# The down products of eight middle FFN groups by seven block products, with weight sums made in DRAM

## The chip, the cores and the metric

The kernel runs on one core of one Trainium2 chip. The metric is the time of one launch on the device, in microseconds (us). All data is float32. Engines are called PE (TensorE), PEld (its weight load), DVE (VectorE), ACT (ScalarE), POOL (GpSimd) and SP (SyncE, which only issues transfers).

## The reference

One encoder layer for two request groups that share the weights: 512 frames of a prompt and 8 x 16 frames of running streams, 640 tokens in all, model width 1024. The layer is an FFN half step, a mixer (short convolution and retention) and a second FFN half step, each followed by a layer norm. The change touches the two FFN half steps alone:

```
def swiglu(x, w_up, w_down):            # D_MODEL 1024, D_FF 2816
    a, b = jnp.split(x @ w_up, 2, axis=-1)
    return (jax.nn.silu(a) * b) @ w_down
x = layer_norm(ALPHA * x + 0.5 * swiglu(x, ffn_w_up, ffn_w_down), ln_g, ln_b)
```

## The kernel before

Every float32 operand of a product is split in a high part and a low part (float32r tiles such as `hh` and `hl`, `wh` and `wl`), and each product is three matmuls into one PSUM bank: high x low, low x high, high x high (`mm3`, L878).

The 22 row tiles of h (128 features by 640 tokens each) go in `GROUPS = (2, 4, 4, 4, 4, 4)`. Each of the five later groups is four quads and then a down stretch. A quad (PE L1130, ACT L1614, DVE L2114) makes two tiles of the up products by seven block products, 84 matmuls of 320 columns: its weights come as `qraw`; POOL makes two sums of them (`sums`, L776); ACT copies the high parts (`wqh`) and DVE subtracts the low parts (`wql`), one quad ahead. ACT and DVE combine the results from PSUM in `ct`, DVE multiplies gate and value to h, ACT copies `hh`, DVE subtracts `hl` and frees PE with `h_ready`.

The down product of a group is 4 row tiles of h (128 features) times 512 x 1024 of the down weights, added into `z` (5 tiles of 128 tokens by 1024). In the middle groups (1 to 4 of each FFN, eight in all) `natural` (L939) makes it in two halves of 512 columns: 10 banks, each summed over 4 k tiles, three matmuls each: 120 matmuls of 512 columns, the stationary operand being a 128 x 128 piece of `hh` or `hl`. Six of them (`lead_down`, L1099) stand in the last quad, to cover a wait there. DVE adds each bank to `z` when it is done (`down`, L2272): five adds after each half. The last group of each FFN and the first (2 tiles) go in other ways.

The down weights come in chunks of 128 x 1024, four a middle group, in a ring of `NSPL = 3` slots of SBUF. A chunk is loaded twice: by SP as `raw`, and by POOL's queue as `wh` with the rounding to float32r (`high`, L754); then POOL subtracts the low part in place (`low`, L764, the instruction is L773). A slot is loaded anew when PE has begun the chunk after the one that it holds (`chunk_used`, inside `mm`, L870). All queues are in the order of the program: POOL's in a middle group is

```
high(ck(3))
for part in range(3):
    sums(2 * k)
    low()
sums(2 * k)
low()
```

so that three chunks are split within the first three quads; the fourth waits for its slot. SP issues `qraw` loads and `raw` loads in one queue (`ffn`, L638).

## Time and profile before

| what | us |
|---|---|
| time, median of 3 runs (lowest, highest) | 1780.93 (1778.66, 1781.36) |
| profiled execution, its span from first to last instruction | 1778.3 |
| PE busy in it | 1766.5 |
| DVE, ACT, POOL busy | 1286.1, 653.3, 551.6 |
| a down stretch of a middle group (first matmul after the quads to first matmul of the next quad) | 25.88 |
| the four quads before it, with the six leading down matmuls | 50.60 |

No time of the profiled execution is listed beside its span; the median of the runs lies 2.6 us above that span. PE's busy time counts matmuls as the profile models them, so it is read beside the starts of single matmuls.

### The profile page before, as it was taken

What the parts mean: (1) busy time and instruction counts of PE and PEld (TensorE: products, weight loads), DVE (VectorE), ACT (ScalarE), POOL (GpSimd) and SP (SyncE); (2) the same over time, 40 slices, a digit from 0 to 9 for tenths busy, and PEclk for the clock granted to TensorE, in tenths of its full rate; (3) what the DMA queues carried; (4) which work ended last, traced back from release to release, by engine and by line L of the source; (5) the groups of instructions that cost most, each with busy time, mean ns of one, the idle gap of its engine ahead of it and who ended that gap; (6) DMA issues with size and microseconds to landing.
All of it is one profiled execution on the core that took longest, in us unless ns stands there. A gap on an engine that the chain in (4) does not pass through costs nothing.

```text
span 1778.3 us, 26857 instructions
## 1 busy us (share of the span) xinstructions
PE 1766.5 (99%) x10776; PEld 1653.0 (93%) x10776; DVE 1286.1 (72%) x1708; ACT 653.3 (37%) x1120; POOL 551.6 (31%) x355
## 2 busy tenths in 40 slices
PE   9999999999999999999999999999999999999998
PEld 9989999898999999999998989898989989899997
DVE  7958485678788787777266777767867968485676
ACT  5425233243545454444105050514224325242343
POOL 3424242242232222221242323332343324233331
PEclk9999999999999999999999999999999999999999
DMA  7442423334443333433674858676963442324223
GB/s 275 136 137 72 143 78 130 126 94 178 148 148 127 115 128 99 139 98 95 243 247 159 313 198 296 214 265 222 351 264 118 129 154 86 131 79 135 90 89 107
DMA packets 87259, 282.61 MB, mean 159 GB/s; under 512 B 8672, under 2 KB 9056, under 8 KB 86880
## 3 DMA queue, kind: packets, MB, share of 16 engines
q1 hardware_dynamic: 48096, 172.77, 29.4%
q10 hardware_dynamic: 24784, 56.21, 8.7%
q0 software_dynamic: 14256, 51.91, 8.6%
q8 instruction: 86, 1.41, 0.3%
q14 instruction: 37, 0.30, 0.1%
HBM read 239.63 MB, written 42.28 MB: 159 GB/s over the span
## 4 chain that ended last, share of the span: by engine, by line
PE 94%; DVE 3%; DMA 1%; ACT 1%; issue 1%; DVEq 0%; ACTq 0%
PE ps L872 93%; PE ps L1348 1%; DMA out_ret_sample<-state 1%; DMA state<-in_state_ret 0%; DVE xl L1961 0%; DVE z L2277 0%; DMA opening<-in_opening 0%; DVE z L2380 0%; PE ps L1257 0%; DVE wql L1961 0%; ACT xh L1510 0%; ACT t L1900 0%; DVE t L2010 0%; DVE y L2415 0%; DVE tl L1961 0%
## 5 line engine op out<-in xcount | busy, mean ns | idle before, releaser
L872 PE MATMUL ps<-th,wql 128*128 128x320 f32 x1136 | 351.0, 309 | 0.0
L872 PE MATMUL ps<-th,wqh 128*128 128x320 f32 x1136 | 350.7, 309 | 0.0
L872 PE MATMUL ps<-tl,wqh 128*128 128x320 f32 x1136 | 350.0, 308 | 0.0
L773 POOL TENSOR_TENSOR wl<-raw,wh 128x1024 fp32r<-128x1024 f32 x100 | 262.8, 2628 | 133.9 <-DMA wh<-in_weights 81.8
L1510 ACT ACTIVATE pu<-ps 128x320 f32<-128x320 f32 x213 | 93.2, 438 | 515.8 <-PE ps L872 515.8
L1961 DVE TENSOR_TENSOR wql<-qraw,wqh 128x512 fp32r<-128x512 f32 x213 | 260.0, 1221 | 17.2 <-ACT wqh L1510 17.0
L872 PE MATMUL ps<-xh,wql 128*128 128x320 f32 x852 | 262.7, 308 | 0.2 <-DVE wql L1961 0.2
L872 PE MATMUL ps<-xl,wqh 128*128 128x320 f32 x852 | 262.7, 308 | 0.0
L872 PE MATMUL ps<-xh,wqh 128*128 128x320 f32 x852 | 262.6, 308 | 0.0
L786 POOL TENSOR_TENSOR quad_s<-qraw 128x512 f32<-128x512 f32 x71 | 96.7, 1362 | 478.8 <-DVE wql L1961 412.9
L1961 DVE TENSOR_TENSOR wql<-quad_s,wqh 128x512 fp32r<-128x512 f32 (+1 forms) x213 | 197.5, 927 | 44.2 <-ACT wqh L1510 43.4
L872 PEld LDWEIGHTS ps<-th,wql 128*128 128x128 f32 x1136 | 213.2, 188 | 0.7 <-ACT pu L1510 0.3
L872 PEld LDWEIGHTS ps<-tl,wqh 128*128 128x128 f32 x1136 | 213.3, 188 | 0.4
L872 PEld LDWEIGHTS ps<-th,wqh 128*128 128x128 f32 x1136 | 213.2, 188 | 0.0
L761 POOL DMA_DIRECT2D wh<-in_weights x92 | 51.7, 563 | 457.1 <-PE ps L872 445.1
L1510 ACT ACTIVATE wqh<-quad_s 128x512 fp32r<-128x512 f32 (+1 forms) x213 | 163.8, 769 | 53.5 <-PE ps L872 50.5
L872 PE MATMUL ps<-wh,hl 128*128 128x512 f32 x420 | 163.8, 390 | 0.1
L872 PE MATMUL ps<-wh,hh 128*128 128x512 f32 x420 | 163.7, 390 | 0.0
L872 PE MATMUL ps<-wl,hh 128*128 128x512 f32 x420 | 163.6, 390 | 0.0
L872 PEld LDWEIGHTS ps<-xh,wql 128*128 128x128 f32 x852 | 159.9, 188 | 1.1 <-DVE wql L1961 0.5
L872 PEld LDWEIGHTS ps<-xl,wqh 128*128 128x128 f32 x852 | 160.0, 188 | 0.4
L872 PEld LDWEIGHTS ps<-xh,wqh 128*128 128x128 f32 x852 | 160.0, 188 | 0.0
(246 smaller groups left out, 3446.2 us busy)
## 6 DMA issues: line engine op xcount, KB each, us to landing
qraw<-in_quads SPq DMA_DIRECT2D x142, 512.0 KB, 3.6
raw<-in_weights SPq DMA_DIRECT2D x100, 512.0 KB, 3.9
wh<-in_weights POOLq DMA_DIRECT2D x92, 512.0 KB, 5.3
state<-in_state_ret ACTq DMA_DIRECT2D x32, 512.0 KB, 7.5
out_ret_sample<-state ACTq DMA_DIRECT2D x32, 512.0 KB, 6.4
state<-in_state_ret SPq DMA_DIRECT2D x16, 512.0 KB, 5.7
qk_scratch<-ctp SPq DMA_DIRECT2D x8, 640.0 KB, 5.6
swish_scratch<-ctp SPq DMA_DIRECT2D x6, 640.0 KB, 2.9
```

The source lines that it names most:

```text
L761: pool.dma_start(w_hi(r), a["weights"][c]).then_inc(hi_loaded[r], 16)
L773: pool.tensor_tensor(w_lo(r), w_raw(r), w_hi(r).bitcast(f32), ALU.subtract).then_inc(chunk_split, 1)
L786: pool.tensor_tensor(qs[:, 0, :], qraw[:, c0, 512:1024], qraw[:, c1, 512:1024], ALU.add).then_inc(pool_sums, 1)
L872: ins = nc.tensor.matmul(out, lhs, rhs, start=start, stop=stop, skip_group_check=adds)
L1348: last = nc.tensor.transpose(cols(k, 128, ps[:, b, :]), src, ident[:, :])
L1510: return nc.scalar.activation(out, in_, ACT.Copy, **kw)
L1961: return V.tensor_tensor(out, x, y, op)
```

## The change

In the middle groups the part of the down product that four of the five token tiles take of the down product is made by seven block products, not eight. Of the four row tiles of h, two form the first row block (features) and two the second; the 512 token columns form two column blocks of 256; the weights of a group form blocks A11, A12 (first 512 output columns, first and second row block) and A21, A22. The fifth token tile (128 tokens) stays out of the seven products: its first half is made with A11 and A12, its second with S1, A22 and one difference `d`. The products take sums of h (`n1`, `n2`, `t3`, `t4`, `d`), which DVE makes (2 x 256 or 2 x 128 columns), ACT rounds to high parts and DVE turns into low parts; and sums of weights S1 to S4, which are made in DRAM: ACT's queue copies four base blocks of 512 KB to a scratch tensor, and POOL's queue adds to them in three accumulating transfers (1 MB, 512 KB, 512 KB), each after the one before has landed.

PE runs 108 matmuls a middle group instead of 120, over seven chunks instead of four, in eight banks, with waits for DVE's reading of a bank between accumulations into it (`down_read`). DVE adds 15 results to `z` instead of 10, between the sums of h. The ring has four slots; the room comes from the scratch of the transfer descriptors, cut from its standard size to 2048. POOL's and SP's orders in a middle group are new. The diff, cut to what the prediction speaks of (indentation reduced):

```diff
-NSPL = 3
+NSPL = 4
...
+SPLIT_GROUPS = range(1, len(GROUPS) - 1)
+SPLIT_CHUNKS = ("A11", "S1", "A12", "S2", "S3", "A22", "S4")
+SUMS_KEPT = ("S1", "S3", "S2", "S4")
+SPLIT_BANKS = 8
+FFN_CHUNKS = 4 + 2 + len(SPLIT_CHUNKS) * len(SPLIT_GROUPS) + 4
...
+        def chunk_source(engine, c):
+    if not is_sum(c):
+        return a["weights"][PLAIN[c]]
+    at, what = split_chunk(c)
+    engine.wait_ge(sums_added[{"S1": 0, "S3": 0, "S2": 1, "S4": 2}[what]], 16 * (at + 1))
+    return a["sums"][at, SUMS_KEPT.index(what)]
...
@@ SP, ffn @@
-        for g in range(1, len(GROUPS)):
+        for g in SPLIT_GROUPS:
+            load(1)
+            load_quad(2 * k)
+            load_quad(2 * k)
+            load(1)
+            load_quad(2 * k)
+            load(2)
+            load_quad(2 * k)
-            load(1)
+            load(3)
...
+    def add_first(at):
+        pool.wait_ge(base_copied, 16 * (at + 1))
+        pool.dma_start(a["sums"][at, 0:2].rearrange("m p d -> (m p) d"),
+                       a["sum_add"][at].rearrange("m p d -> (m p) d"), accum_op=ALU.add,
+                       max_dma_last_dim=4 * D).then_inc(sums_added[0], 16)
+    def add_next(at, step):
+        pool.wait_ge(sums_added[step - 1], 16 * (at + 1))
+        pool.dma_start(a["sums"][at, step + 1], a["sums"][at, 0 if step == 1 else 2], accum_op=ALU.add,
+                       max_dma_last_dim=4 * D).then_inc(sums_added[step], 16)
...
@@ GpSimd, ffn @@
+        for g in SPLIT_GROUPS:
+            at = split_after(k, g)
+            high(ck(1))
+            sums(2 * k)
+            add_first(at)
+            low()
+            sums(2 * k)
+            add_next(at, 1)
+            high(ck(2))
+            sums(2 * k)
+            add_next(at, 2)
             high(ck(3))
             low()
+            sums(2 * k)
+            low()
+            low()
+            high(ck(2))
+            low()
+            high(ck(2))
+            low()
+            low()
...
+    def split_lead():
+        pe.wait_ge(h_ready, hr(2))
+        s, b0 = chunk(), bk.at
+        pe.wait_ge(psum_free, b0 + 3 - 7)
+        for kk in range(2):
+            last = mm3(ps[:, (b0 + 3) % 8, :], (hh[:, kk, 0:128], hl[:, kk, 0:128]),
+                       (cols(kk, 512, w_hi(s)), cols(kk, 512, w_lo(s))), kk == 0, kk == 1)
+        last.then_inc(down_full, 1)
+        return s
+    def split_down(led, h0):
+        at, b0 = split_done.at, bk.at
+        y_at, o1, x_at, o2, w_at = (0, 1), 2, (3, 4), 5, (6, 7)
+        def product(s, place, left, start):
+            if start:
+                pe.wait_ge(psum_free, b0 + place - 7)
+            for kk in range(2):
+                last = mm3(ps[:, (b0 + place) % 8, :], (left[0](kk), left[1](kk)),
+                           (cols(kk, 512, w_hi(s)), cols(kk, 512, w_lo(s))), start and kk == 0, kk == 1,
+                           adds=not start)
+            return last
...
+        product(led, x_at[1], of_h(0, 1), True).then_inc(down_full, 1)
+        product(led, o1, of_h(0, 2), True)
+        owed[0] = True
+        s = chunk()
+        summed(1)
+        for q in range(2):
+            product(s, w_at[q], of_sum(n1h, n1l, q), True).then_inc(down_full, 1)
+        product(s, o2, of_h(0, 2), True)
+        owed[0] = True
+        s = chunk()
+        pe.wait_ge(h_ready, h0 + 4)
+        for q in range(2):
+            product(s, y_at[q], of_h(2, q), True).then_inc(down_full, 1)
+        product(s, o1, of_h(2, 2), False).then_inc(down_full, 1)
+        owed[0] = True
+        s = chunk()
+        summed(2)
+        for q in range(2):
+            read(1 + q)
+            product(s, x_at[q], of_sum(n2h, n2l, q), False).then_inc(down_full, 1)
+        owed[0] = True
+        s = chunk()
+        summed(3)
+        for q in range(2):
+            read(5 + q)
+            product(s, x_at[q], of_sum(t3h, t3l, q), False).then_inc(down_full, 1)
+        owed[0] = True
+        s = chunk()
+        summed(5)
+        for q in range(2):
+            read(7 + q)
+            product(s, x_at[q], of_sum(t4h, t4l, q), False).then_inc(down_full, 1)
+        product(s, o2, of_sum(dh, dl, 0), False).then_inc(down_full, 1)
+        owed[0] = True
+        s = chunk()
+        for q in range(2):
+            last = product(s, w_at[q], of_h(2, 3 + q), False)
+            if q == 0:
+                last.then_inc(down_full, 1)
+        last.then_inc(psum_full, SPLIT_BANKS)
+        owed[0] = True
+        bk.add(SPLIT_BANKS)
+        split_done.add()
...
+    def base_copy(at):
+        if at:
+            act.wait_ge(sums_added[0], 16 * at)
+        act.dma_start(a["sums"][at].rearrange("m p d -> (m p) d"),
+                      a["sum_base"][at].rearrange("m p d -> (m p) d")).then_inc(base_copied, 16)
+    def split_his(n):
+        ts_hi_part(n2h, n2f)
+        ts_hi_part(t3h[:, :, :], t3f[:, :, :])
+        ts_hi_part(dh[:, :, :], df[:, :, :])
+        act.wait_ge(h_ready, 2 * (stage_of(n) // 2 + 1) + 2 * (ffn_index(n) // 2 + 1))
+        ts_hi_part(t4h, t4f[:, :, :])
...
@@ ScalarE, quad and ffn @@
...
+        if split_quad(n) and local(n) % 4 == 2:
+            ts_hi_part(n1h[:, :, :], n1f[:, :, :])
...
+        if ends and split_quad(n):
+            split_his(n)
...
+                if q == 2 and g in SPLIT_GROUPS and split_after(k, g) < 2 * len(SPLIT_GROUPS) - 1:
+                    base_copy(split_after(k, g) + 1)
...
+    def ts_lo_part(out, f, hi):
+        ts.add()
+        dve.wait_ge(ts_hi, ts())
+        tt(out, f, hi.bitcast(f32), ALU.subtract).then_inc(ts_ready, 1)
+    def first_difference(n):
+        dve.wait_ge(h_summed, ffn_index(n) // 2)
+        summed_of_h(tt(n1f[:, :, :], h32_first, h32_second, ALU.subtract))
...
+        def out_of(place, t, half, last, sign=1.0):
+            if place == "w1" and last:
+                dve.wait_ge(psum_full, b0 + SPLIT_BANKS)
+            else:
+                seen.add()
+                dve.wait_ge(down_full, seen())
+            zt = cols(half, 512, z[:, t, :])
+            ins = V.scalar_tensor_tensor(out=zt, in0=ps[:, (b0 + places[place]) % 8, :], scalar=sign * scale,
+                                         in1=zt, op0=ALU.mult, op1=ALU.add)
+            if last:
+                ins.then_inc(psum_free, 1)
+            else:
+                read.add()
+                ins.then_inc(down_read, 1)
...
+        dve.wait_ge(h_summed, ffn_index(n) // 2 + 1)
+        summed_of_h(V.scalar_tensor_tensor(out=n2f, in0=n1f[:, :, :], scalar=-1.0, in1=h32_second,
+                                           op0=ALU.mult, op1=ALU.subtract))
+        h_lo_part(n)
+        out_of("x0", 0, 0, False)
+        out_of("x1", 1, 0, False)
+        step(tt(t3f[:, :, :], h32_second, b12[0], ALU.subtract))
+        dve.wait_ge(ts_summed, 5 * at + 2)
+        step(V.scalar_tensor_tensor(out=t4f[:, :, :], in0=n2f, scalar=-1.0, in1=h32_first,
+                                    op0=ALU.mult, op1=ALU.subtract))
+        after()
+        ts_lo_part(n2l, n2f, n2h)
+        out_of("w0", 3, 1, False, -1.0)
+        out_of("w1", 4, 1, False, -1.0)
+        summed_of_h(tt(t3f[:, :, :], t3f[:, :, :], b12[1], ALU.subtract))
+        step(tt(odd_pieces(df[:, :, :]), h32_odd, odd1[0], ALU.subtract))
+        out_of("y0", 0, 0, True)
+        after()
+        summed_of_h(tt(odd_pieces(df[:, :, :]), odd_pieces(df[:, :, :]), odd1[1], ALU.subtract))
+        summed_of_h(V.memset(mv[:, TT, 0:1], 0.0))
+        ts_lo_part(t3l[:, :, :], t3f[:, :, :], t3h[:, :, :])
+        out_of("y1", 1, 0, True)
+        out_of("o1", 2, 0, True)
+        out_of("x0", 3, 0, False)
+        ts_lo_part(dl[:, :, :], df[:, :, :], dh[:, :, :])
+        out_of("x1", 4, 0, False)
+        ts_lo_part(t4l, t4f[:, :, :], t4h)
+        z_settled()
+        out_of("x0", 3, 1, False, -1.0)
+        out_of("x1", 4, 1, False, -1.0)
+        z_settled()
+        out_of("x0", 0, 1, True, -1.0)
+        out_of("x1", 1, 1, True, -1.0)
+        out_of("o2", 2, 1, True)
+        out_of("w0", 3, 0, True)
+        out_of("w1", 4, 0, True)
+        assert (seen.at, read.at) == (15 * at + 15, 8 * at + 8)
+        bk.add(SPLIT_BANKS)
+        dve.wait_ge(psum_free, bk())
+        split_done.add()
     def quad(n):
...
@@ VectorE, quad @@
...
+            if split_quad(n):
+                first_difference(n)
...
+        if split_quad(n) and local(n) % 4 == 2:
+            ts_lo_part(n1l[:, :, :], n1f[:, :, :], n1h[:, :, :])
...
+        if ends and split_quad(n):
+            split_evacuations(n)
         if prepares:
             quad_lo_part(n + 1, A22)
             quad_lo_part(n + 1, S4)
-        if ends and not projects:
+        if ends and not projects and not split_quad(n):
             h_lo_part(n)
...
-            if g < len(GROUPS) - 1:
-                down(0.5 / ALPHA, 0)
-                down(0.5 / ALPHA, 1)
...
+    elif f0 + tiles < FT:
+        part = quarters(down, f0)
+        for what in SPLIT_CHUNKS:
+            if what[0] == "A":
+                out.append(part[what])
+        bases.append([part[of] for of in ("A21", "A21", "A11", "A12")])
+        added.append([part[of] for of in ("A22", "A11")])
...
-    nc = bacc.Bacc("TRN2", target_bir_lowering=False, num_devices=1)
+    nc = bacc.Bacc("TRN2", target_bir_lowering=False, num_devices=1, dynamic_dma_scratch_size=2048)
```

The chunks of a group come in the order A11, S1, A12, S2, S3, A22, S4. `down_full` counts PE's block results, `down_read` DVE's reads of banks that PE adds to again, `ts_summed`, `ts_hi` and `ts_ready` the sums of h, their high parts and their low parts. `base_copy` of the next group is issued by ACT after the third quad of a group.

## Rows read from the trace of the kernel before

**Rows 1.** The page's first part: busy us, share, instructions of each engine.

```profile
PE 1766.5 (99%) x10776; PEld 1653.0 (93%) x10776; DVE 1286.1 (72%) x1708; ACT 653.3 (37%) x1120; POOL 551.6 (31%) x355
```

**Rows 2.** The page's chain that ended last, by engine.

```profile
PE 94%; DVE 3%; DMA 1%; ACT 1%; issue 1%; DVEq 0%; ACTq 0%
```

**Rows 3.** Windows: stretch, busy us of each engine, granted clock, transfers' share, GB/s.

```profile
124.83:175.43 50.60, 50.60 (x343) 50.34 (x342) 40.41 (x42) 24.72 (x42) 19.90 (x12) 1.00 0.30 92
175.43:201.31 25.88, 25.88 (x117) 21.41 (x116) 11.46 (x16) 2.00 (x3) 4.96 (x5) 1.00 0.47 155
...
430.76:1372.58 941.82, 940.02 (x5890) 880.80 (x5888) 685.80 (x1017) 350.47 (x619) 284.05 (x179) 1.00 0.56 191
```

**Rows 4.** Timeline of PE (start, us, instruction) at both ends of that down stretch.

```profile
175.28 0.31 PE L872 MATMUL ps<-xh,wqh 128*128 128x320 f32 x1
175.43 0.39 PE L872 MATMUL ps<-wh,hl 128*128 128x512 f32 x1
...
201.31 0.32 PE L872 MATMUL ps<-xh,wql 128*128 128x320 f32 x1
```

**Rows 5.** Timeline of DVE and of ACT about the start of that down stretch.

```profile
173.93 0.68 DVE L1961 TENSOR_TENSOR wql<-quad_s,wqh 128x512 fp32r<-128x512 f32 x1
174.54 0.68 DVE L1961 TENSOR_TENSOR quad_s<-quad_s,qraw 128x512 f32<-128x512 f32 x1
175.69 0.82 DVE L1961 TENSOR_TENSOR ct<-pu,ps 128x640 f32<-128x640 f32 x1 [0.47 <-issue]
176.54 1.49 DVE L1961 TENSOR_TENSOR ct<-ct,ct 128x1280 f32<-128x1280 f32 x1
...
178.07 1.37 ACT L1510 ACTIVATE hh<-ct 128x640 fp32r<-128x640 f32 x2 [1.80 <-DVE ct L1961]
...
179.16 1.56 DVE L1961 TENSOR_TENSOR hl<-ct,hh 128x640 fp32r<-128x640 f32 x2
```

**Rows 6.** Timeline of POOL about the same start.

```profile
172.17 1.29 POOL L786 TENSOR_TENSOR quad_s<-qraw 128x512 f32<-128x512 f32 x1 [5.04 <-DVE wql L1961]
174.69 1.68 POOL L790 TENSOR_TENSOR quad_s<-qraw 128x512 f32<-128x512 f32 x1 [1.23 <-DVE wql L1961]
181.59 0.57 POOL L761 DMA_DIRECT2D wh<-in_weights  x1 [5.23 <-PE ps L872]
```

**Rows 7.** Timeline of POOL and of DVE, both at work in a quad.

```profile
75.30 2.86 POOL L773 TENSOR_TENSOR wl<-raw,wh 128x1024 fp32r<-128x1024 f32 x1
...
76.65 2.86 DVE L1961 TENSOR_TENSOR ct<-ct,ct 128x1280 f32<-128x1280 f32 x1
```

**Rows 8.** Timeline of POOL and of DVE, both at work in a down stretch.

```profile
105.12 0.58 POOL L761 DMA_DIRECT2D wh<-in_weights  x1 [5.01 <-PE ps L872]
109.89 2.39 POOL L773 TENSOR_TENSOR wl<-raw,wh 128x1024 fp32r<-128x1024 f32 x1 [4.19 <-DMA wh<-in_weights]
...
108.71 3.41 DVE L2277 SCALAR_TENSOR_TENSOR z<-ps,z 128x512 f32<-128x512 f32 x5 [3.87 <-PE ps L872]
```

**Rows 9.** DMA issues of the page: count, KB each, median us to landing.

```profile
qraw<-in_quads SPq DMA_DIRECT2D x142, 512.0 KB, 3.6
raw<-in_weights SPq DMA_DIRECT2D x100, 512.0 KB, 3.9
wh<-in_weights POOLq DMA_DIRECT2D x92, 512.0 KB, 5.3
...
out_y_prompt<-in_ln_b ACTq DMA_DIRECT2D x1, 1024.0 KB, 7.4
out_y_prompt<-y POOLq DMA_DIRECT2D x2, 512.0 KB, 6.9
```

**Rows 10.** Timelines of ACT, DVE and POOL within quads.

```profile
159.86 0.48 DVE L1961 TENSOR_TENSOR ct<-pu,ps 128x320 f32<-128x320 f32 x1
...
162.00 0.44 ACT L1510 ACTIVATE ct<-ps 128x320 f32<-128x320 f32 x1 [0.86 <-PE ps L872]
...
147.04 1.29 POOL L786 TENSOR_TENSOR quad_s<-qraw 128x512 f32<-128x512 f32 x1 [6.49 <-DVE wql L1961]
```

**Rows 11.** Timeline of PE at both ends of the kernel, and the window after it.

```profile
1.26 4.58 PE L872 MATMUL ps<-ones 128*128 128x320 f32 x16 [1.26 <-DVE ones L2470]
...
1769.76 0.39 PE L872 MATMUL ps<-wh_x,hh 128*128 128x512 f32 x1
...
1771.00:1774.00 3.00, 0.00 (x0) 0.00 (x0) 2.72 (x8) 1.54 (x3) 0.00 (x0) 0.96 0.86 341
```

More of the change, by code:

```diff
@@ L60, with split_chunk, is_sum, split_after @@
 RELEASES = release_order()
+def split_chunk(c):
+    for k, at in enumerate((0, CHUNKS - FFN_CHUNKS)):
+        n = c - at - FIRST_UNITS - 2
+        if 0 <= n < len(SPLIT_CHUNKS) * len(SPLIT_GROUPS):
+            return len(SPLIT_GROUPS) * k + n // len(SPLIT_CHUNKS), SPLIT_CHUNKS[n % len(SPLIT_CHUNKS)]
+    return None
+def is_sum(c):
+    return split_chunk(c) is not None and split_chunk(c)[1][0] == "S"
+PLAIN = [sum(not is_sum(e) for e in range(c)) for c in range(CHUNKS)]
+def split_after(k, g):
+    return len(SPLIT_GROUPS) * k + g - 1
+def group_banks(g):
+    return SPLIT_BANKS if g in SPLIT_GROUPS else 2 * TT
+def split_quad(n):
+    return stage_of(n) != 1 and local(n) // 4 + 1 in SPLIT_GROUPS
 def released(c):
@@ L117 @@
 PROJ = QUAD_START[1]
-PROJ_BANKS = 2 * 4 + 3 * QUADS + 2 * TT * len(GROUPS) + 2 * TT + 2 * 4
+PROJ_BANKS = 2 * 4 + 3 * QUADS + sum(group_banks(g) for g in range(len(GROUPS))) + 2 * TT + 2 * 4
 HEADS_BANKS = PROJ_BANKS + 3 * len(PROJECTIONS) + 1 + 2 * 2 + 2 * KT
@@ L495, in build_layer @@
         sig_made, h_summed, h_hi = sem("sig_made"), sem("h_summed"), sem("h_hi")
+        base_copied = sem("base_copied")
+        sums_added = [sem(f"sums_added{n}") for n in range(3)]
+        down_full, down_read = sem("down_full"), sem("down_read")
+        ts_summed, ts_hi, ts_ready = sem("ts_summed"), sem("ts_hi"), sem("ts_ready")
         t_summed, t_hi, t_ready = sem("t_summed"), sem("t_hi"), sem("t_ready")
@@ L1237, in ffn @@
                         first_down()
-                    elif g < len(GROUPS) - 1:
-                        for half in range(2):
-                            natural(tiles // 2, hh, hl, lambda k: pe.wait_ge(h_ready, h0 + k + 1),
-                                    led=None if half else led)
+                    elif g in SPLIT_GROUPS:
+                        split_down(led, h0)
                     else:
@@ L2744, in weight_chunks, with quarters @@
 def weight_chunks(ffn1_up, ffn1_down, w_in, w_conv, w_ret, w_out, ffn2_up, ffn2_down):
-    out = []
+    out, bases, added = [], [], []
+    def quarters(w, f0):
+        return {f"A{d}{k}": tiled(w[(f0 + 2 * k - 2) * 128:(f0 + 2 * k) * 128, (d - 1) * 512:d * 512], 512)
+                for d in (1, 2) for k in (1, 2)}
     def tiled(w, cols):
@@ L2787, in weight_chunks @@
     ffn(ffn2_up, ffn2_down)
-    return np.stack(out)
+    return np.stack(out), np.array(bases), np.array(added)
 def kernel(x_prompt, x_sample, cache_conv, state_ret, ln1_g, ln1_b, ffn1_w_up, ffn1_w_down, w_in, conv_w,
```

101 lines of the change are left out of this document (76 added, 25 removed).

## The prediction

> **What bounds the kernel now.** The page's first part shows PE busy for 1766.5 of 1778.3 us [rows 1], and the chain of waits ends in PE for 94% of the span [rows 2]. The windows say that this holds in every stage that the change touches: in the four quads of a middle group and in its down stretch PE is busy for 50.60 of 50.60 and 25.88 of 25.88 us, at the full granted clock [rows 3]. So matmuls taken away are worth their full time, and so is every wait put in. The same windows give the reserve of the others: in the down stretch DVE works 11.5 of 25.9 us, ACT 2.0, POOL 5.0; in the quads DVE works 40.4 of 50.6. The kernel waits for nothing there, and the question is whether DVE and POOL, which get the new work in the stretch where PE gets shorter, still keep ahead.
>
> **PE's own work.** A down stretch has 114 matmuls of 512 columns between 175.43 and 201.31 [rows 4]: 25.88 / 114 = 0.227 us each. The change takes 12 of 120 away: 2.72 us a group, 21.8 us in eight groups. Counted from the start of the stretch (T), with no wait, PE would begin S1 at 2.7, A12 at 6.8, S2 at 10.9, S3 at 13.6, A22 at 16.3, S4 at 20.4 and end at 23.2 (12, 18, 18, 12, 12, 18, 12 matmuls).
>
> **DVE and POOL hold each other up.** POOL's low part took 2.39 us beside DVE's adds from PSUM, which also ran on at 3.41 / 5 = 0.68 us each [rows 8]. In a quad it was otherwise: POOL's low part began at 75.30 and took 2.86, and DVE's product of two SBUF tiles, issued at 76.65, took 2.86 instead of the 1.49 of the same product at 176.54 [rows 5, 7]. 76.65 + 2.86 - 1.49 = 78.02, when POOL's 75.30 + 2.86 = 78.16 was nearly over. So a DVE instruction with two SBUF inputs waits for a running POOL subtraction, the other way round as well (POOL's 1.68 against 1.29 of the sister sum [rows 6]), and an add from PSUM doesn't.
> This trace agrees with the Trainium skill ("SBUF — State Buffer", section "Who interferes with whom"), which says that a DVE instruction with two SBUF inputs and a GpSimd one that reads SBUF exclude each other for the whole instruction.
>
> **Where POOL now works.** Before, three low parts lie in the quads and POOL is idle from 176.37 to 181.59 [rows 6], just when DVE makes the last two tiles of h [rows 5]. After, the order is sums, low A12, low S2 with nothing to wait for between: sums end at T + 0.9 (176.37 - 175.43), since their second half waits for DVE's subtraction at 173.93 [rows 5, 6]; then two low parts of 2.4 us, alternating with DVE:
> - DVE's product for h needs 1.4 us (176.54 to 177.95 before); it gets in before or behind the first low part and h is there at T + 3.1 to 4.7 instead of 2.5.
> - the new difference n2 (0.61, the distance of the starts at 173.93 and 174.54 [rows 5]) waits for the end of one low part, then DVE's two `hl` subtractions (0.72 each) for the end of the other. Low parts end at about 5.4 and 8.4, so h is ready at 8.4 + 1.5 = 9.9. PE wants it at 6.8: wait 3.1 us. Before it was ready at 180.71 - 175.43 = 5.3 [rows 5].
>
> **DVE's chain to S3.** PE may add S3's products only after DVE has read x0 the second time (`down_read` 5). After `hl` stand eight adds to z (8 x 0.67), five operations on 512 columns (t3 twice, t4, low parts of n2 and t3: 5 x 0.61), two on 256 (0.33 each) and 0.2 of small things: 5.4 + 3.0 + 0.7 + 0.2 = 9.3 us of work, and T + 19.2. In it fall POOL's low S3 and low A22 (the wh transfer is issued at about 8.4, behind the low parts, and lands 4.8 later [rows 8]): 0 to 2.4 us each. Laying the instructions of DVE, POOL, ACT and PE in order with these durations I get 1.1 + 2.4: S3 begins at 22.7 instead of 13.6. The remaining adds keep up with PE, since they come one per 1.36 us of matmuls. Net a group: 9.1 of waits (3.1 before A12, 6.0 before S3) less 2.7 is +6.4 us. The same laying out gives 76.45 a group for the old order, where the trace has 50.60 + 25.88 = 76.48, and DVE's and POOL's starts within 0.3 us. With landings between 4.6 and 6.5 us it gives +6.1 to +9.3; with neither of the last two low parts in the way, +2.8.
>
> **The clock.** A wait of 6 us is new: in this trace the granted clock fell once, after the last matmul at 1769.76 (mean 0.96 in 1771 to 1774), and the first 16 matmuls took 4.58 us, 0.286 each where later ones of the same shape take 0.147: the lower level, 1.2 GHz of 2.4 [rows 11]. So PE's clock may fall before S3; one fall by these rows costs half of 4.58 = 2.3 us. I count half of it, 1.15 us a group (bounds 0 and 2.3).
> The Trainium skill ("TensorE: Matmul & The Clock Gate", section "HAM oscillation — how this bites in real kernels") says that waits of this kind return in every round with their slow matmuls; by it the full price would stand in every group, the second rival below. The trace of before can't show it, as its waits in the groups are none.
>
> **What else is added, counted at nothing.** ACT: five roundings (5 x 0.6 us) in an engine that works 2.0 of 25.9 us, hidden. Third quad: DVE gets n1 and its low part, 1.2 us, ACT 0.54; DVE's result for the last product stands 2.1 us ahead of the copy that comes just before PE's need [rows 10], so 0, at most 0.7 us a group (5 in all). Weight traffic: seven chunks of twice 0.5 MB instead of four, 2 MB of copies and 2 MB of accumulation, in all 8.4 MB -> 15 to 17 MB a group, 113 -> about 200 GB/s; the middle of the kernel moves 191 GB/s with PE at 940 of 942 us [rows 3], so hidden. The three accumulating transfers stand one quad (12.3 us) or more apart; the nearest rows are 6.9 us (accumulating, 0.5 MB) and 7.4 us (1 MB within DRAM) [rows 9], and POOL, which waits for each, is idle 6.5 us before its sums [rows 10]. Held up behind POOL's wait are its sums, and behind SP's wait for S2 the fourth `qraw` load: hidden until a link takes some 19 us. The fourth slot and the smaller scratch: between -3 and +3 us elsewhere, taken as 0.
>
> **Sum.** 8 x (6.4 + 1.15) = +60 us on a span of 1778.3: 1838. The median of the runs is 2.6 above this span: **1841**. This case alone reaches from 8 x 2.8 = +22 (1803) to 8 x (9.3 + 2.3) = +93 (1874).
>
> **Rivals.**
> - *DVE keeps ahead, the change gains* (17%). If the low parts fall on DVE's adds from PSUM, which they don't disturb [rows 8], DVE's work from T to `down_read` 5 is about 14.0 us against PE's 13.6: 0.5 us lost, 2.2 gained a group, 8 x 2.2 = 17.6, **1763**. For it: POOL's lows are 4 x 2.4 in 22 us, DVE's adds leave holes for them. Against: POOL's queue puts two of them on the tiles of h, and no add can be moved there. It decides below 2.7 us of waits a group.
> - *The clock falls at both waits of every group* (11%): 8 x (6.4 + 2 x 2.3) = +88, **1869**. For: the waits are longer than before by far. Against: 3.1 and 6.0 us are short, and only the end of the kernel shows a fall at all.
> - *The accumulating transfers are slow* (6%). If the first takes 25 us, POOL stands 25 - 13.6 = 11.4 us, of which 6.5 are idle time; 4.9 us later reach PE's next quad in every group: 8 x (7.55 + 4.9) = +100, **1881**. For: they read and write the same DRAM and nothing like them is in the trace. Against: 6.9 us for half the size.
> - *Both effects cancel* (4%): waits of just 2.7 us, **1781**.
>
> **How the numbers follow.** The likeliest case has 62%. All cases but the first and last rivals are slower: 79%; within 0.2% (3.6 us, what a measurement of this kernel can tell from none) 4%; faster 17%. The range 1790 to 1875 leaves out the faster case, the even one and part of the slow transfers, and cuts nothing of the likeliest.
>
> **What would show it.** PE's idle time in a middle group by releaser: before the first matmul of A12 a wait for `hl`, about 3 us, and before S3 a wait for a DVE add to z, about 6 us; POOL's wl subtractions right after its last sum, and DVE instructions with two SBUF inputs of 2 to 3 us beside them; 10,680 matmuls; the granted clock in the down stretch below 1.00 if it falls. Down stretches of 23 to 24 us would prove me wrong, as would waits that stand in the quads and not in the down stretch (transfers), or sums of h that don't slow down beside POOL.

## The result and the profile after

The changed kernel takes 1879.8 us (median of 4 runs, 1873.2 to 1880.6) against 1780.2 before (median of 4): **ratio 1.0554, 95% interval 1.0537 to 1.0572**. It is slower by 5.5%. The prediction was 1841 with a range of 1790 to 1875: the direction was right, the size was not, and the time lies outside the range. The profiled execution has a span of 1877.9 us at a mean granted clock of 0.979 (before 1778.3 at 0.999).

The page's first part (busy us, share, instructions), and its chain that ended last:

```profile
PE 1786.2 (95%) x10680; PEld 1654.4 (88%) x10680; DVE 1445.9 (77%) x1860; ACT 674.4 (36%) x1160; POOL 641.2 (34%) x427
...
PE 19%; DVE 10%; DMA 2%; issue 2%; ACT 1%; POOL 0%; DVEq 0%; POOLq 0%; ACTq 0%
```

PE has the 96 matmuls fewer that were counted, 10,680 instead of 10,776 [rows 1], and is yet busy 19.7 us longer: matmuls at the lower clock take longer. DVE is busy 160 us longer. Its new instructions alone make 63 of these (1349.3 us busy in experiment 5, where nothing holds them up, against 1286.1 before); the rest is time in which an instruction of DVE counts as busy and stands held up by POOL. The chain of before was PE for 94% [rows 2]; now it is followed for a third of the span only and goes through DVE and a load of `qraw`.

The windows of the stages [rows 3]: the quads of the second middle group, its down stretch, the down stretch of the last middle group, and the middle of the kernel (busy us of each engine, granted clock, transfers' share, GB/s):

```profile
140.44:191.18 50.74, 50.74 (x343) 50.34 (x342) 40.93 (x45) 25.12 (x43) 17.48 (x14) 1.00 0.70 203
191.18:229.04 37.86, 27.39 (x105) 21.05 (x103) 28.85 (x31) 4.20 (x7) 18.71 (x11) 0.91 0.44 146
1762.09:1793.13 31.04, 25.35 (x105) 19.92 (x103) 27.30 (x32) 4.20 (x7) 18.60 (x12) 0.95 0.59 178
483.36:1429.29 945.93, 942.56 (x5890) 881.77 (x5888) 702.67 (x1017) 350.63 (x619) 280.21 (x178) 1.00 0.55 191
```

Before, a down stretch took 25.88 us with PE always busy; now this one takes 37.86, and PE stands for 10.5 of them. The eight stretches together take 298.1 us instead of 207.0: **+91.1 of the 99.6 us of span**. The middle of the kernel gives +4.1 (945.9 against 941.8), the quads and the rest +4.4. The 91.1 are taken apart by the starts of the matmuls: gaps of more than 0.24 us beyond a matmul's own time (waits) sum to 85.1 us, matmuls that start late by 0.06 to 0.24 us (those at the low clock, called slow matmuls below) to 26.3, 1.5 are small delays, and the twelve matmuls fewer per group take 21.8 away.

**Where PE waits.** PE's waits by releaser (us in total, times, longest):

```profile
PE ps L983 <- DVE z L2372: 36.5, 8, 7.3
PE ps L983 <- DVE ct L2187: 26.9, 9, 4.7
```

The first row is the predicted wait before S3, for DVE's adds to z, eight times. The second wasn't predicted: seven times PE waits 3.2 to 4.9 us (27.6 together) before S1, the second block product, because DVE hasn't read out the last quad's banks (`ct`). T is again the start of the stretch. Timeline of DVE in the stretch that starts at 191.18 (start, us, instruction, idle time before it and its releaser):

```profile
189.78 0.69 DVE L2187 TENSOR_TENSOR wql<-quad_s,wqh 128x512 fp32r<-128x512 f32 x1
195.10 1.73 DVE L2187 TENSOR_TENSOR quad_s<-quad_s,qraw 128x512 f32<-128x512 f32 x1 [4.63 <-POOL quad_s L878]
196.76 0.81 DVE L2187 TENSOR_TENSOR ct<-pu,ps 128x640 f32<-128x640 f32 x1
197.60 2.80 DVE L2187 TENSOR_TENSOR ct<-ct,ct 128x1280 f32<-128x1280 f32 x1
200.44 2.79 DVE L2387 SCALAR_TENSOR_TENSOR ct<-n1f,ct 128x512 f32<-128x512 f32 x1
...
207.13 2.77 DVE L2187 TENSOR_TENSOR n2r<-ct,n2r 128x512 fp32r<-128x512 f32 x1
```

and of POOL in the same stretch:

```profile
193.80 1.26 POOL L878 TENSOR_TENSOR quad_s<-qraw 128x512 f32<-128x512 f32 x1 [9.43 <-DMA qraw<-in_quads]
195.03 1.26 POOL L882 TENSOR_TENSOR quad_s<-qraw 128x512 f32<-128x512 f32 x1
196.24 6.43 POOL L852 TENSOR_TENSOR wl<-raw,wh 128x1024 fp32r<-128x1024 f32 x2
...
206.47 2.89 POOL L852 TENSOR_TENSOR wl<-raw,wh 128x1024 fp32r<-128x1024 f32 x1 [0.37 <-DMA wh<-sums_scratch]
```

Read them together. POOL's sums, which stood at T - 3.3 before [rows 6], start at T + 2.6, since POOL waits 9.4 us for a load. DVE's second sum waits for them, and the read-out of the banks stands behind it in DVE's queue. Then mutual exclusion of DVE's instructions with two SBUF inputs and POOL's subtractions, as predicted: beside POOL's two low parts (6.43 us for two) DVE's product takes 2.80 instead of 1.49 us and the difference n2 2.79 instead of 0.68; beside the third, which begins at 206.47, the low part of n2 takes 2.77.

**The late load.** Transfers: the issues of the page (KB each, median us to landing), and the same for 184 to 186 us alone, where that load is issued:

```profile
qraw<-in_quads SPq DMA_DIRECT2D x142, 512.0 KB, 3.7
...
sums_scratch<-in_sum_add POOLq DMA_DIRECT2D x8, 1024.0 KB, 10.0
```

```profile
qraw<-in_quads SPq DMA_DIRECT2D x1, 512.0 KB, 8.7
```

and for 178 to 190 us:

```profile
sums_scratch<-sums_scratch POOLq DMA_DIRECT2D x1, 512.0 KB, 12.1
wh<-sums_scratch POOLq DMA_DIRECT2D x1, 512.0 KB, 13.2
sums_scratch<-in_sum_base ACTq DMA_DIRECT2D x1, 9.4
```

The 2 MB base copy for the next group is issued at 179.31, the third accumulation at 180.5 and the load of S2, the result of the second, at 181.1. The second half of the fourth `qraw` load follows at 184.96 and lands after 8.7 us instead of 3.6 [rows 9]. It is also issued late, at T - 6.2; before it was T - 7.7. SP waits there for a subtraction of DVE, which POOL's low part of S1 holds up. DVE and then POOL at that time:

```profile
181.76 3.17 DVE L2187 TENSOR_TENSOR wql<-qraw,wqh 128x512 fp32r<-128x512 f32 x1
```

```profile
181.66 2.71 POOL L852 TENSOR_TENSOR wl<-raw,wh 128x1024 fp32r<-128x1024 f32 x1
```

The last group has no copy beside it, and fits this: no wait before S1, 31.04 us, with 3.1 us before A12 (predicted 3.1) and 2.7 before S3. Experiments 2 and 3 test it.

### The profile page after: what moved, and what is told of

Its sections match the earlier page's. It is cut to its first block and busy times, and to the rows that moved or that the text cites. A ratio compares the mean times of both kernels' runs of the same rounds, so it can differ in the third digit from the quotient of the medians.

```text
span 1877.9 us, 27089 instructions
## 1 busy us (share of the span) xinstructions
PE 1786.2 (95%) x10680; PEld 1654.4 (88%) x10680; DVE 1445.9 (77%) x1860; ACT 674.4 (36%) x1160; POOL 641.2 (34%) x427
## 3 DMA queue, kind: packets, MB, share of 16 engines
q0 software_dynamic: 22192, 81.27, 15.7%
## 5 line engine op out<-in xcount | busy, mean ns | idle before, releaser
L852 POOL TENSOR_TENSOR wl<-raw,wh 128x1024 fp32r<-128x1024 f32 x124 | 327.4, 2644 | 146.3 <-DMA wh<-in_weights 48.8
L878 POOL TENSOR_TENSOR quad_s<-qraw 128x512 f32<-128x512 f32 x71 | 98.0, 1380 | 605.8 <-DVE wql L2187 386.8
L983 PE MATMUL ps<-xh,wqh 128*128 128x320 f32 x852 | 262.6, 308 | 0.0
L2187 DVE TENSOR_TENSOR wql<-qraw,wqh 128x512 fp32r<-128x512 f32 x213 | 249.8, 1173 | 0.4
L2187 DVE TENSOR_TENSOR quad_s<-quad_s,qraw 128x512 f32<-128x512 f32 x138 | 114.2, 827 | 54.7 <-POOL quad_s L878 47.7
L882 POOL TENSOR_TENSOR quad_s<-qraw 128x512 f32<-128x512 f32 x71 | 112.5, 1584 | 73.4 <-DVE wql L2187 73.4
L1705 ACT ACTIVATE wqh<-qraw 128x512 fp32r<-128x512 f32 x213 | 132.8, 624 | 10.4 <-PE ps L983 10.4
```

The lines of the kernel that those rows point to most:

```text
L852: pool.tensor_tensor(w_lo(r), w_raw(r), w_hi(r).bitcast(f32), ALU.subtract).then_inc(chunk_split, 1)
L878: pool.tensor_tensor(qs[:, 0, :], qraw[:, c0, 512:1024], qraw[:, c1, 512:1024], ALU.add).then_inc(pool_sums, 1)
L882: pool.tensor_tensor(qs[:, 2, :], qraw[:, c0, 0:512], qraw[:, c0, 512:1024], ALU.add).then_inc(pool_sums, 1)
L983: ins = nc.tensor.matmul(out, lhs, rhs, start=start, stop=stop, skip_group_check=adds)
L1705: return nc.scalar.activation(out, in_, ACT.Copy, **kw)
L2187: return V.tensor_tensor(out, x, y, op)
```

## The experiments

Times are medians with the ratio to the kernel before (1779 to 1780 us on the same chip) and its 95% interval. "Stretches" are the eight down stretches together (before 207.0, after 298.1).

**1. DVE's second sum behind the bank read-out.** In the fourth quad `second_sum` moves behind the products of h.

```
-                    second_sum(n + 2)
+                    if not (ends and split_quad(n)):
+                        second_sum(n + 2)
...
                 if not ends_stage_at(n, 2):
+                    if ends and split_quad(n):
+                        second_sum(n + 2)
                     fourth_sum(n + 2)
```

> In the last quad of a split group DVE's sum for the quad after next (it waits for POOL's sums) is moved behind the reading out of the banks. Theory 1 (POOL's last sums of a group come 4 us late, because their qraw load is late, and DVE stands in front of the last quad's bank until they come): the wait before the S1 products (3.2 to 4.9 us in seven groups, 27.6 us in all) goes, with it one of the two falls of the clock; low parts of A12 and S2 still come late and hold DVE, so about 34 us a down stretch instead of 37.3: 1850 us, between 1838 and 1862. Rival (the S1 wait is set by something else, the bank or the n1 parts): within 5 us of 1880.

1835.2 us, 1.0318 [1.0299, 1.0337], 3 us under the expected range; stretches 257.3. The wait before S1 is gone in all eight groups. Before A12 it is 2.3 to 2.8, before S3 1.5 to 7.3 us. So this queue order carries 45 us of the loss. That is more than the S1 waits (27.6 us), since the waits before S3 got shorter too. What ends these is not always DVE: PE's waits of this kernel, and POOL's low part of S3 in the second group (T = 182.53):

```profile
PE ps L983 <- POOL wl L852: 28.4, 13, 3.0
PE ps L983 <- DVE z L2372: 17.9, 6, 7.2
```

```profile
199.84 2.35 POOL L852 TENSOR_TENSOR wl<-raw,wh 128x1024 fp32r<-128x1024 f32 x1 [4.98 <-DMA wh<-sums_scratch]
```

In five of the eight groups S3 starts when this low part ends (here at T + 19.7; DVE's second reading of x0 had ended at T + 18.6). Its chunk is issued only behind POOL's two low parts, and POOL waits 5.0 us for the landing. So POOL's own lateness is a second way in which its low parts cost time, beside the hold on DVE. (Before A12 the first row names POOL too, but there DVE's `hl` ends later: T + 9.0 against 8.4, with A12 at 9.1.)

**2. The base copy in four pieces, one a quad.**

```
-                if at:
-                    act.wait_ge(sums_added[0], 16 * at)
-                act.dma_start(a["sums"][at]..., a["sum_base"][at]...).then_inc(base_copied, 16)
+                if at > 1:
+                    act.wait_ge(sums_added[0], 16 * (at - 1))
+                act.dma_start(a["sums"][at, m], a["sum_base"][at, m]).then_inc(base_copied[at % 2], 16)
...
```

> The 2 MB base copy of the next group is issued as four copies of 512 KB, one behind each quad, instead of one behind the third. Theory 1 (the copy and the accumulation beside it hold up the qraw load): POOL's last sums are on time, the S1 wait goes in all groups, down stretches are as the one group without a copy, 31 us instead of 38: 7 x 7 = 49 us less, 1831, between 1822 and 1848. Rival (it is SP's queue, where the qraw load stands behind the S2 chunk that waits for an accumulation, and not the bytes in flight): nothing changes, 1875 to 1885.

1860.2 us, 1.0462 [1.0441, 1.0483]; stretches 267.4. A miss by 12 us over the range: the wait before S1 did shrink to 0 to 0.8 us and the stretches are 31 us shorter, but the span outside the stretches grew by 8 us beside the changed kernel's. PE's waits of this kernel name a new one:

```profile
PE ps L983 <- DVE z L2372: 29.0, 9, 5.2
...
PE ps L983 <- ACT pu L1705: 12.1, 12, 1.3
```

Its DVE and POOL before the fourth quad:

```profile
179.14 3.90 DVE L2187 TENSOR_TENSOR wql<-qraw,wqh 128x512 fp32r<-128x512 f32 x1
182.96 0.81 DVE L2187 TENSOR_TENSOR ct<-pu,ps 128x640 f32<-128x640 f32 x1
```

```profile
176.13 1.28 POOL L878 TENSOR_TENSOR quad_s<-qraw 128x512 f32<-128x512 f32 x1 [9.18 <-DMA qraw<-in_quads]
...
179.78 2.70 POOL L852 TENSOR_TENSOR wl<-raw,wh 128x1024 fp32r<-128x1024 f32 x1
```

Here the third `qraw` load is later: POOL's sum starts 38.7 us after the quads did, 35.9 in the changed kernel. POOL's low part of S1 comes later in its quad and holds a DVE subtraction for 3.90 us; the read-out behind it, ACT's copies behind that and PE follow (1.1 us of wait for `pu`). Spreading a transfer had moved the collision, not removed it. The rival, that the `qraw` load stands behind SP's wait for an accumulation and not behind bytes in flight, foretold no change and is out.

**3. No sums: plain chunks in place of the summed ones, no base copies, no accumulation** (the summed weights are left out of the computation).

```
-            at, what = split_chunk(c)
-            engine.wait_ge(sums_added[...], 16 * (at + 1))
-            return a["sums"][at, SUMS_KEPT.index(what)]
+            return a["weights"][PLAIN[c]]
...
```

> The base copies and accumulating transfers are left out, and plain chunks are loaded in place of the sums (the down products are not those of the reference). Theory 1 and any theory that blames transfers: S1 waits go, 31 us a down stretch or a little less, 1829, between 1820 and 1840; what is left of waits, about 6 us a group before A12 and S3, is DVE held up by POOL. Theory 2 (only DVE and POOL holding each other up matters): 1880 as before. If the transfers were all of the loss: 23.2 us a stretch, 1762.

1846.4 us, 1.0384 [1.0367, 1.0402], a miss by 6 us over the range; stretches 273.8, nearly equal in all groups: 1.9 us before A12, 1.0 before S2, 5.3 before S3, 8.5 in all. The transfers, with the waits of SP and POOL for them, carry 33 us: 24 in the stretches and 9 elsewhere. Of the 9 some 4 are in the middle of the kernel, where the changed kernel is longer by 4.1 and this one is not; no run shows why. POOL's low parts and the clock are left, 67 us above the kernel before. Set against the prediction it is the kernel that was in fact predicted: 8.5 us of waits a group against 9.1, and 1846 us against 1841. That the sums come so near is partly luck, since the slow matmuls are 19.4 us here (2.4 a group), all but 1.3 of them behind the last wait, where I had counted 1.15 a group.

**4. POOL writes zeros instead of the low parts of the split groups** (they are left out). A write without an input in SBUF, 0.95 us.

```
-                pool.tensor_tensor(w_lo(r), w_raw(r), w_hi(r).bitcast(f32), ALU.subtract).then_inc(chunk_split, 1)
+                if split_chunk(c):
+                    pool.memset(w_lo(r).bitcast(f32), 0.0).then_inc(chunk_split, 1)
+                else: ...
```

> POOL writes zeros in place of the low parts of the down chunks of the split groups (the low parts of these weights are left out), with the same waits and signals; the instruction reads nothing from SBUF. Theory 2 (a POOL subtraction and a DVE instruction with two SBUF inputs exclude each other): the waits before A12 and S3 go, the S1 wait from the late qraw load stays with one fall of the clock: 28 to 30 us a down stretch, 1806 to 1822 us. DVE's instructions on two SBUF inputs in the down stretch take 0.4 to 1.5 us each, none 2 to 3. Rival (DVE's chain is long by its own work, or waits for PE and ACT): 36 us or more a stretch, above 1860.

1801.7 us, 1.0130 [1.0115, 1.0145], 4 us under the expected range; stretches 227.4. The wait before A12 is gone in all groups, that before S3 in all but two (1.5 and 0.8 us). In the last group (no copy) these 0.8 us are all that PE waits:

```profile
1690.96:1715.11 24.15, 23.55 (x105) 19.07 (x103) 19.74 (x31) 4.10 (x7) 8.27 (x12) 1.00 0.71 237
```

In the other groups the wait before S1 stays:

```profile
PE ps L986 <- DVE ct L2190: 24.1, 7, 4.5
PE ps L986 <- DVE z L2375: 2.0, 2, 1.4
```

Compared with this, the subtractions cost 78 us, more than any other part. The run takes out two things at once: the hold on DVE, and 1.4 us or more of POOL's own time in each low part (0.95 instead of 2.35 at the least), on which the next chunk's issue waits (experiment 1). The hold is seen by itself in DVE's rows: at the same place of the second group the product takes 1.49 us here and the difference n2 0.69, where they took 2.80 and 2.79. How the 78 us divide between the two isn't shown.

**5. Both: no sums and no low parts** (both left out; the edits of experiments 3 and 4).

> No copies and accumulations for the sums (plain chunks in their place) and POOL's writing of zeros in place of the low parts of the split groups' chunks: neither the late qraw load nor POOL's hold on DVE is left, PE's and DVE's instructions are those of the change. If the loss is made of these two and the clock that falls in their waits: 24.2 us a down stretch as in the one group of the memset kernel that has no copy, 8 x 1.7 = 14 us less than before, 1765, between 1760 and 1770. If DVE's own longer chain or the eight banks cost something by themselves: 1780 or more.

1760.8 us, 0.9894 [0.9881, 0.9908]; stretches 188.1. The same window as above in the second group:

```profile
172.63:196.08 23.45, 23.45 (x104) 19.09 (x103) 18.83 (x30) 4.10 (x7) 7.17 (x10) 1.00 0.64 202
```

PE waits in two groups for 0.3 to 0.4 us before S3 and else never, and its clock stays at 1.00 in the stretches. All of DVE's new work, and the roundings on ACT, are hidden. The gain of the arithmetic is real, 19 us, and the whole loss of the change lies in the two things taken out here.

**6. The fourth slot and the smaller scratch alone, in the kernel before.**

```
-NSPL = 3
+NSPL = 4
...
-    num_devices=1)
+    num_devices=1, dynamic_dma_scratch_size=2048)
```

> The kernel before with nothing changed but four chunk slots and the smaller scratch for transfer descriptors. My sum took this at 0 (-3 to +3 us): 1777 to 1782. If the smaller scratch or the other slots cost the 4 us that the middle of the kernel (mixer) is longer by after the change: 1783 or more.

1780.7 us, 1.0014 [1.0005, 1.0023]: 2.5 us by the ratio, between 0.9 and 4.1 (the medians differ by 1.7; three of the eleven runs took 1784 to 1785). It was taken as 0 with 3 either way; at most a small part of the loss.

**7. Experiments 1 and 2 together.**

> Both mends of the late qraw load together: the copy in four pieces and DVE's sum behind the reading out. If the S1 wait is gone with either, the two don't add up: only the lock between DVE and POOL and one fall of the clock are left, 29.5 to 31 us a down stretch: 1819, between 1812 and 1832. If they mended different things: 1880 - 45 - 20 = 1815 as well or less, so this run tells little between them; it gives the best that the change reaches without touching POOL's low parts, and whether that is still above 1779.

1838.9 us, 1.0329 [1.0307, 1.0351]; stretches 247.5, 10 us shorter than in experiment 1, but PE waits 15.7 us for `pu` in the quads (6.0 there). No better than experiment 1, and a miss by 7 us over the range for the same reason as experiment 2.

**8. Keeping the clock up: 20 products of ones before S1, 40 before S3** (they alter results). The first filling stands before S1, where the wait for the bank read-out is, not before A12.

```
                 product(led, o1, of_h(0, 2), True)
                 owed[0] = True
+                idle_products(20, b0 % 8)
...
                 owed[0] = True
+                read(4)
+                for _ in range(40):
+                    mm(ps[:, (b0 + 6) % 8, 0:HALF], ones[:, 0:128], ones[:, :], False, False, True)
```

> The changed kernel with 20 matmuls of ones (2.9 us) put into the wait before S1 and 40 (5.9 us) into the wait before S3 (the latter add to a bank of results, so the down products are not the reference's). Theory 3 (the clock falls in these waits and the slow matmuls after cost time): the low level is hardly granted any more in the down stretches (72 us before), the 26 us of slow matmuls go, of which some part was hidden behind DVE's chain; 10 to 26 us less: 1854 to 1870. Rival (the slow matmuls were hidden behind DVE anyway, and the extra matmuls only take time): 1880 to 1895.

1878.3 us, 1.0550 [1.0534, 1.0566]. The low level is left for 20 instead of 72 us of the stretches, and the time is the same (the stretches too: 298.4 against 298.1). The second group's stretch:

```profile
189.12:227.51 38.39, 33.93 (x164) 28.86 (x163) 29.02 (x31) 4.20 (x7) 18.53 (x11) 0.96 0.43 138
```

The fillings are 60 x 0.147 = 8.8 us a group and partly longer than the waits that they fill (the last group, which has no wait before S1, went from 31.0 to 32.4 us), so equal times don't say that the clock is free: waits and fillings together grew by 17 us (31.5 and 70.6 against 85.1), and slow matmuls fell by nearly as much (9.8 against 26.3). The trace of the changed kernel can be read further: of its 26.3 us of slow matmuls 14.9 stand ahead of another wait of the same stretch and 11.4 behind the last one, 1.4 us a group. In the second group DVE waits for nothing from 195.10 until S3 has begun, so the slow matmuls in between don't hold it up; POOL waits once for PE there, 2.4 us, so this is a reading and no proof. By it only the 11.4 are on the path. In experiment 3, with one fall a group and no wait behind it, it is 18.1 of 19.4 us, 2.3 a group.

**9. The same with short fillings, on the kernel of experiment 1** (12 before A12, 12 before S3; they alter results).

```
                 owed[0] = True
+                for _ in range(12):
+                    mm(ps[:, (b0 + 0) % 8, 0:HALF], ones[:, 0:128], ones[:, :], False, False, True)
                 s = chunk()
                 pe.wait_ge(h_ready, h0 + 4)
...
```

> The kernel with the second sum late (1835 us; low level for 44 us of its down stretches, 16.1 us of slow matmuls), and 12 products of ones more in each of its two waits per group, before A12 (wait 2.3 to 2.8 us) and before S3 (2 to 7 us): 12 x 0.147 = 1.8 us each, less than either wait, so they delay nothing. They alter the results. If the slow matmuls add to the time, their 16 us come back: 1819 us (1815 to 1824). If they are hidden, because DVE's chain and not PE decides when S3 may start, the time stays within 4 us of 1835. The first try at this had its first filling before S1 and longer than the wait, and could not tell.

1859.3 us (1848.8 to 1867.1), 1.0443 [1.0401, 1.0485]: slower by 24 us than experiment 1, which neither theory had. The profiled run is the fastest, 1848.8; in it the low level fell from 44 to 27 us. DVE in the first group's stretch, here and then in experiment 1:

```profile
115.47 0.68 DVE L2377 SCALAR_TENSOR_TENSOR z<-ps,z 128x512 f32<-128x512 f32 x1
116.07 2.03 DVE L2192 TENSOR_TENSOR df<-df,hl 128x256 f32<-128x256 f32 x1
118.03 3.25 DVE L2192 TENSOR_TENSOR t3l<-t3f,t3h 128x512 fp32r<-128x512 f32 x1
```

```profile
114.74 0.68 DVE L2372 SCALAR_TENSOR_TENSOR z<-ps,z 128x512 f32<-128x512 f32 x1
115.34 0.42 DVE L2187 TENSOR_TENSOR df<-df,hl 128x256 f32<-128x256 f32 x1
115.68 0.69 DVE L2187 TENSOR_TENSOR t3l<-t3f,t3h 128x512 fp32r<-128x512 f32 x1
...
116.29 1.88 DVE L2372 SCALAR_TENSOR_TENSOR z<-ps,z 128x512 f32<-128x512 f32 x3
```

and POOL's low part of S3, in the same order:

```profile
115.42 2.39 POOL L852 TENSOR_TENSOR wl<-raw,wh 128x1024 fp32r<-128x1024 f32 x1 [2.82 <-DMA wh<-sums_scratch]
...
118.36 2.36 POOL L852 TENSOR_TENSOR wl<-raw,wh 128x1024 fp32r<-128x1024 f32 x1
```

```profile
116.76 2.35 POOL L852 TENSOR_TENSOR wl<-raw,wh 128x1024 fp32r<-128x1024 f32 x1 [4.88 <-DMA wh<-sums_scratch]
```

Up to the first of these rows both chains of DVE are alike, shifted by 0.7 us with the start of the stretch. In experiment 1 the landed chunk lets POOL start at 116.76 (T + 17.2), beside the three adds from PSUM, which still take 0.63 each. Here it starts at 115.42 (T + 15.2), and two subtractions of DVE that stand ahead of the read-out for S3 take 5.3 instead of 1.1 us; S3 begins at T + 23.0 instead of T + 19.6. The price of the exclusion is a matter of two microseconds of phase. That would also explain why waits before S3 range from 1.5 to 7.3 us within one kernel, and why this one's runs spread by 1%; neither is shown. What the clock costs can't be read from these fillings; I leave it at the 11.4 us counted above; no run shows them.

**10. DVE makes the low parts of A12 and S2** (on the kernel of experiment 1).

```
                     sums(2 * k)
-                    low()
-                    low()
+                    low_by_vector()
+                    low_by_vector()
...
                 h_lo_part(n)
+                chunk_low_part(at, 2)
...
                 ts_lo_part(n2l, n2f, n2h)
+                chunk_low_part(at, 3)
```

> The kernel with the second sum late (1835 us, stretches of 32.2 us), and in it DVE instead of POOL makes the low parts of A12 and S2 in the down stretches; POOL still makes those of A11, S1, S3, A22 and S4. Theory (mutual exclusion): the two subtractions cost DVE 2 x 1.2 us (1024 columns at the rate of the 1.49 us for 1280), but nothing holds the tiles of h, n2 and hl up any more, so the wait before A12 goes, and the wait before S3 is (14.0 + 2.4) - 13.6 = 2.8 us, up to 5.2 with one low part still in the way: stretches of 26.2 to 28.6 us, 1835 - 8 x 4.8 = 1797 us (1788 to 1806). Rival (the waits come from DVE having too much work and late operands, not from POOL): two more subtractions on DVE make every wait longer by 2.4 us, 1835 + 19 = 1854 us.

1846.4 us, 1.0372 [1.0354, 1.0389], 11 us slower than experiment 1; stretches 266.4 against its 257.3. Between the theories, nearer to the rival's 1854, and both missed: the wait before A12 fell to 0 to 1.4 us, but that before S3 is 6.2 us (8.4 once). DVE and POOL in the second group:

```profile
195.84 1.22 DVE L2192 TENSOR_TENSOR wl<-raw,wh 128x1024 fp32r<-128x1024 f32 x1
196.98 1.28 DVE L2388 SCALAR_TENSOR_TENSOR z<-ps,z 128x512 f32<-128x512 f32 x2
198.18 1.92 DVE L2192 TENSOR_TENSOR t3f<-t3f,hl 128x512 f32<-128x512 f32 x1
200.02 2.72 DVE L2192 TENSOR_TENSOR df<-ct,hh 128x256 f32<-128x256 f32 x1
```

```profile
197.15 2.40 POOL L852 TENSOR_TENSOR wl<-raw,wh 128x1024 fp32r<-128x1024 f32 x1 [2.96 <-DVE wl L2192]
...
200.09 2.35 POOL L852 TENSOR_TENSOR wl<-raw,wh 128x1024 fp32r<-128x1024 f32 x1
```

DVE pays 2 x 1.2 us of work, and POOL's low parts of S3 and A22, left where they were, now hit two short DVE instructions for 3.5 us more. I had allowed for one of them. Two subtractions less on POOL didn't help while two others stayed beside DVE's chain.

**11. POOL's low parts of A12 and S2 ahead of its last sums** (on the changed kernel).

```
                     high(ck(3))
                     low()
-                    sums(2 * k)
                     low()
                     low()
+                    sums(2 * k)
```

> The changed kernel with POOL's two low parts of A12 and S2 ahead of its last sums in the fourth quad, instead of behind them. Mutual exclusion: they then fall in the quad and no longer on the tiles of h; the wait before A12 goes and that before S3 gets shorter, stretches of about 31.5 us instead of 37.3; but they wait for the chunks to land, and the sums behind them are later by 3 to 5 us, which the bank read-out behind DVE's second sum passes on to PE: about 1880 us (1865 to 1895), no gain. If only the order on POOL mattered and its sums had slack: 1880 - 8 x 5.8 = 1834 us.

1862.5 us (1855.1 to 1869.9), 1.0465 [1.0432, 1.0497]; stretches 262.6 in the profiled run, the slowest of the four. The wait before A12 is gone, that before S1 stays in seven groups (1.1 to 4.2 us), and the span outside the stretches is 26 us longer than the changed kernel's, with waits of PE there instead. One DVE subtraction in a quad, and the first of two low parts in a row on POOL (the second ends at 183.76):

```profile
178.06 6.26 DVE L2187 TENSOR_TENSOR wql<-qraw,wqh 128x512 fp32r<-128x512 f32 x1
```

```profile
178.68 2.71 POOL L852 TENSOR_TENSOR wl<-raw,wh 128x1024 fp32r<-128x1024 f32 x1
```

35 us gained in the stretches, 26 given back; the median is 2.5 us under the expected range, and still far above the kernel before.

## Why the prediction was wrong in size and right in direction

- **PE's own work** (21.8 us saved): right. 10,680 matmuls, and 19 us shorter when nothing else interferes (experiment 5).
- **DVE and POOL hold each other up**: right. The rows show it, experiments 4 and 5 its price together with POOL's own time. The held durations are near those named: 2.8 us for a product of 1.49, POOL's low part up to 3.7 (2.35 when nothing holds it). The Trainium skill ("SBUF — State Buffer", section "Who interferes with whom") says that a DVE instruction with two SBUF inputs contends with a GpSimd one that reads SBUF, and one with at most one SBUF input, outside its 2-port modes, does not. The rows agree: the adds, whose other input is in PSUM, take 0.63 us each beside POOL (experiment 9).
- **DVE's chain to S3** (3.1 + 6.0 = 9.1 us of waits a group): close. 8.5 without the transfers (experiment 3: 1.9 + 5.3, and 1.0 before S2 for POOL's low part, which wasn't predicted), 5.9 in the last group of the changed kernel. In the other groups part of it hides behind the wait before S1.
- **The clock** (1.15 us a group): underrated. In the case that was predicted (experiment 3) it falls once in every group and costs 2.3 us, the upper bound. In the changed kernel the level of 1.2 GHz holds for 72 us of the stretches, after two waits in each but the last, and slow matmuls sum to 3.3 us a group; 1.4 of them are behind the last wait. The Trainium skill ("TensorE: Matmul & The Clock Gate", section "HAM oscillation — how this bites in real kernels") is borne out in that the falls return in every round. That each is paid in full is so in experiment 3; in the changed kernel the later wait, which DVE's chain ends, seems to swallow the first one (by the reading in experiment 8, not shown by a run).
- **The failed step: "What else is added, counted at nothing", its weight traffic "so hidden".** It compared GB/s of a whole stage with GB/s of another (203 now in the quads, about as forecast), and a mean says nothing of one load. The 2 MB copy, the third accumulation and two loads are in flight together in the fourth quad, and the one load with a deadline lands after 8.7 us instead of 3.6. I did name what stood behind POOL's and SP's waits, but priced only the links of the accumulation (12.1 us, under the 19 at which they would matter), not the neighbour's landing, and didn't follow POOL's sums to DVE's second sum and the bank read-out behind it: that chain became 5.9 us later in the second group (sums at T + 2.6 instead of T - 3.3), and PE waits 3.8 of them. Its price is 33 us (experiment 3) to 41 (experiment 4 against 5). Moving one DVE instruction gives back all of it (experiment 1, 45 us), with some microseconds more from shorter waits before S3.
- With that step at 33 us, the sum is 1841 + 33 = 1874 against 1880. The signs that I named for transfers would have missed it: I looked for waits in the quads, and this wait stands in the down stretch, behind DVE's queue.
- **The rivals.** "The accumulating transfers are slow" said 1881, and that it meets 1880 is luck: none takes 25 us (the first 10.0 in the median), and no quad starts late. It had only the right kind of resource. "The clock falls at both waits" had the falls right in seven groups, but not their price. "DVE keeps ahead" failed as POOL's low parts fell on the tiles of h.

## What to carry to other kernels

Work put on POOL beside DVE's critical chain is priced by DVE's two-input instructions that it meets, and which it meets hangs on a landing time: sum the worst case, not the mean, or move those operations where DVE only reads PSUM. A large transfer without a deadline still needs a place in time, since it delays the small one that has a deadline; look for the load that is issued behind it (here 5.7 us later), and follow that landing through every queue. In an in-order queue, what waits for a transfer belongs behind what the busiest engine needs: one instruction so moved was worth 45 us.

## What the runs showed of the hardware that was not expected

- A 2 MB copy within DRAM lands after 9.4 us. Beside it and an accumulation (0.5 MB, 12.1 us), a 0.5 MB load on another queue took 8.7 us instead of 3.6.
- One DVE subtraction of 0.69 us took 3.90 us beside a single low part of 2.70 us, and 6.26 us beside two (experiments 2 and 11). Each time it had started 0.6 us before POOL's first low part by the trace, while POOL was issuing transfers, and yet ended after POOL's last: with POOL's instructions back to back DVE doesn't always get in between.
- Waits of 2.7 to 7.5 us lowered the granted clock to 1.2 GHz in every group, and twice in seven of eight. Keeping it up with empty products left the time as it was (1878.3 against 1879.8 us), but waits and products together were 17 us longer than the waits had been, so the price of the clock stays open between 1.4 us a group (counted) and the full 3.3.
